# Routing from the raw residual: norm weights moved into the router's, the root into the selection, GpSimd multiplies x by the gain

## The chip, the cores and the metric

The kernel runs on one core of a Trainium2 chip. The metric is the device time in microseconds of one execution, as the median of several runs; lower is better. PE is TensorE (PEld its weight loads), DVE is VectorE, ACT is ScalarE, POOL is GpSimd, SP is SyncE, which issues most DMAs.

## The reference

Two layers on x (256 tokens x 1024, fp32). Layer 0: pooling mixer and dense SwiGLU. Layer 1: forgetting attention and a mixture of 8 experts, top 2. Each sub-layer has a norm before and one after.

```python
def rms_norm(x, g):
    return x * lax.rsqrt(jnp.mean(x * x, axis=-1, keepdims=True) + RMS_EPS) * g

def moe_swiglu(h, w_router, w_gate, w_up, w_down):
    logits = (h @ w_router).astype(jnp.float32)
    top_val, top_idx = lax.top_k(logits, 2)
    top_w = jax.nn.softmax(top_val, axis=-1)
    gates = jnp.sum(jax.nn.one_hot(top_idx, 8) * top_w[..., None], axis=-2)
    for e in range(8):                      # F_EXP = 3584
        out = out + gates[..., e:e + 1] * swiglu(h, w_gate[e], w_up[e], w_down[e])

# layer 1
x = x + rms_norm(forgetting_attention(rms_norm(x, g[1, 0]), ...), g[1, 1])
x = x + rms_norm(moe_swiglu(rms_norm(x, g[1, 2]), ...), g[1, 3])
```

## The kernel before

Tokens are two blocks (`tb`) of 128, one token a partition. Every engine runs its own program, written out by hand; engines wait for each other on counting semaphores. Weights come in units of 1 MB (128 x 2048 fp32) through a ring: 10 slots up to the experts, 14 with them. SP issues a unit's load when the unit that was in its slot has been used (`unit_used`, `b_used`). Products of most stages are made of three fp32r products: ACT copies a unit to its high part (`hi`, L620), DVE subtracts it from the unit for its low part (`lo`, L931), and PE multiplies high by high, high by low and low by high (`three`, L1413 to L1415). Activations are split likewise.

The experts are taken in four pairs. In a pair, expert A has up to 128 gathered tokens and works with the three products; expert B has up to 64 and works in plain fp32 (L1786, L1799) on unsplit units. A run over an expert is 42 units. SP's first 14 expert units are loaded ahead of the stage below (the last two when x is complete, `x_done` 6).

The stage that the change touches lies between attention and the first expert:

- `out_part` (PE) makes the attention's output in four PSUM banks, two halves of 512 columns for each block. `post_squares(5, tb)` (ACT) squares and sums them, `scale_bank` (DVE) multiplies by the gain, `root` (DVE, a chain of small linked instructions) makes the reciprocal root of the mean square, `add_normed` adds to x (`x_done`).
- `squares(6, tb)`, `root(6, tb)` and `norm_x(6, tb)` make the normed and weighted input `xn`; PE transposes it (`input_transposed(3, tb)`, L1435), ACT and DVE make `h_hi` and `h_lo`. DVE does block 0's `root(6, 0)` and `norm_x(6, 0)` ahead of block 1's post norm.
- The router: 24 products with `wr2` (weights split in high and low) as the stationary side and both blocks' tokens as the moving one give transposed logits, which DVE copies (L1238) and PE transposes back (L1721). DVE takes the top two, makes 0/1 matrices `m12` and `mboth`; PE counts ranks by products with constant matrices (L1727 to L1731); DVE writes `sel`, a 0/1 matrix of tokens by places (L1267), and PE gathers the first expert's tokens with it (`gather`, L1739), `xn` being the stationary side.
- ACT and DVE split the gathered tokens (`he_hi` L827, `he_lo` L1274). DVE then makes the table that orders the experts (`key` to `rtab_i`, L1280 to L1291), and GpSimd the places of all tokens and, once in each half of a pair, the next selection (`select`). GpSimd also loads the gains and clears `y`.
- `keep_warm(n)` (L1420) issues n products of 128 x 128 that nobody reads; the counts are in `WARM`.

Of the kernel before, what the change touches and what calls it, by code (L numbers as in the profile page):

```python
# [24 lines left out]
E = 8  # L25
# [25 lines left out]
SELECT_STEPS = 10  # L51
# [15 lines left out]
WARM = (16, 6, 10, 8, 28, 8, 8, 8)  # L67


def select(eng, ops, chain, before, gpos, gpos_next, step, gate, sel, sel2, gsel, iota, ready,  # L70
           ready_count, done, ALU):
# [15 lines left out]
    ops.tensor_tensor(sel[:, :, :], sel[:, :, :], sel2[:, :, :], ALU.add).then_inc(ready, 1)  # L87
    eng.wait_ge(ready, ready_count)
# [26 lines left out]
def trunk(nc, x_d, norm_g, pool_w, pool_scale, w_in, b_f, w_out, ffn_gate, ffn_up, ffn_down,  # L115
# [9 lines left out]
    with ExitStack() as ctx:  # L125
# [13 lines left out]
        xn = sb("xn", [P, TB, D])  # L139
        h_hi = sb("h_hi", [P, KB, T], f32r)  # L140
        h_lo = sb("h_lo", [P, KB, T], f32r)
# [26 lines left out]
        wr2 = sb("wr2", [P, KB, 2 * E], f32r)  # L168
# [72 lines left out]
        lgT = act[0:E, 0:T]  # L241
# [67 lines left out]
        lgT_psum = sem("lgT_psum")  # L309
        lgT_done = sem("lgT_done")  # L310
# [6 lines left out]
        pairs_done = sem("pairs_done")  # L317
        rank_copied = sem("rank_copied")
# [131 lines left out]
        def sq_at(n, tb):  # L450

            if n == 0:
                return tb + 1
            if n == 7:
                return 20 + 2 * tb + 2
            before, pre = 2 + 6 * ((n - 1) // 2), n % 2 == 0
            if n < 3:
                return before + (4 + tb + 1 if pre else 2 * tb + 2)
            return before + 3 * tb + (3 if pre else 2)
# [36 lines left out]
        def _(sp):  # L496
# [10 lines left out]
            for i, row in enumerate((norm_g[0, 0:1, :], pool_scale, norm_g[0, 1:2, :])):  # L507
# [11 lines left out]
                         w_router[0].rearrange("(k p) n -> p k n", p=P)).then_inc(small_in, 16)  # L519
            sp.dma_start(bf[:, :], b_f.rearrange("o h -> h o")).then_inc(small_in, 16)  # L520
# [94 lines left out]
        def _(sc):  # L615
# [9 lines left out]
            def squares(n, tb):  # L625

                if n:
                    sc.wait_ge(x_done, n - 2 + tb + 1)
                nc.scalar.activation(xn[:, tb, :], x[:, tb, :], ACT.Square,
                                     accum_out=sums[:, n, tb, 0:1]).then_inc(sq_done, 1)  # L630
# [67 lines left out]
            sc.wait_ge(small_in, 48)  # L698
            nc.scalar.activation(wf2[:, :, 0:H], small_w[:, :, 0:H], ACT.Copy).then_inc(small_hi, 1)
            nc.scalar.activation(wr2[:, :, 0:E], small_w[:, :, H:H + E], ACT.Copy).then_inc(small_hi, 1)  # L700
# [118 lines left out]
            sc.wait_ge(gap_done, 1)  # L819
            nc.scalar.activation(gtmp[:, :, 1:2], gtmp[:, :, 0:1], ACT.Exp).then_inc(gexp_done, 1)  # L820
            nc.scalar.activation(silu[:, 0:1], consts[:, C_ONES:C_ONES + 1], ACT.Silu)
# [8 lines left out]
            he_hi(0)  # L830
            hi(MOE_U0 + 3)
# [88 lines left out]
        def _(ve):  # L920
# [13 lines left out]
            def lo(u):  # L934
                split_lo(hi_slot(u), slot_of(u), u + 1 - WHOLE_UNITS)

# [138 lines left out]
            for i, (wide, at, n) in enumerate(((wf2, 0, H), (wr2, H, E))):  # L1075
                ve.wait_ge(small_hi, i + 1)
                nc.vector.tensor_tensor(wide[:, :, n:2 * n], small_w[:, :, at:at + n], wide[:, :, 0:n].bitcast(f32),
                                        ALU.subtract).then_inc(small_lo, 1)
# [72 lines left out]
            ve.wait_ge(small_in, 48)  # L1151
# [86 lines left out]
            nc.vector.tensor_copy(lgT, bank[4][0:E, 0:T]).then_inc(lgT_done, 1)  # L1238
            ve.wait_ge(lg_psum, 1)
            link(nc.vector.tensor_copy(lg[:, :, :], bank[5][:, 0:TB * E].rearrange("p (b e) -> p b e", e=E)))  # L1240
            for tb in range(TB):
                step = nc.vector.max(top[:, tb, :], lg[:, tb, :])
            link(step)
            for tb in range(TB):
                step = nc.vector.max_index(topi[:, tb, :], top[:, tb, :], lg[:, tb, :])
            link(step)
            link(nc.vector.tensor_copy(topf[:, :, :], topi[:, :, 0:2]))
            nc.vector.tensor_tensor(gtmp[:, :, 0:1], top[:, :, 1:2], top[:, :, 0:1], ALU.subtract).then_inc(gap_done, 1)
            for tb in range(TB):
                for i in range(2):  # L1250
                    step = nc.vector.tensor_scalar(m12[:, tb, i, :], iota8, topf[:, tb, i:i + 1], None, ALU.is_equal)
            link(step)
            nc.vector.tensor_tensor(mboth[:, :, :], m12[:, :, 0, :], m12[:, :, 1, :], ALU.add).then_inc(m_done, 1)
            ve.wait_ge(m_done, 1)
            link(nc.vector.tensor_scalar(away[:, :, :], mboth[:, :, 0:1], float(-2 * T), float(2 * T),
                                         ALU.mult, ALU.add))
            ve.wait_ge(gexp_done, 1)
            link(nc.vector.tensor_scalar(gtmp[:, :, 2:3], gtmp[:, :, 1:2], 1.0, None, ALU.add))
            link(nc.vector.reciprocal(gate[:, :, 0:1], gtmp[:, :, 2:3]))
            link(nc.vector.tensor_tensor(gate[:, :, 1:2], gate[:, :, 0:1], gtmp[:, :, 1:2], ALU.mult))  # L1260
# [3 lines left out]
            count = bank[5][:, TB * E:(TB + 1) * E]  # L1264
# [143 lines left out]
        def _(pe):  # L1408
# [276 lines left out]
            def out_part(w, tb):  # L1685
                hi, lo = weights(OUT_U0 + w, D)
                tok = slice(tb * P, (tb + 1) * P)
                for half in range(2):
                    cols = slice(half * HALF, (half + 1) * HALF)
                    for i in range(2):  # L1690
                        k = 2 * w + i
                        step = three(bank[(3, 7, 1, 2)[2 * tb + half]][:, :], o_hi[:, k, tok], o_lo[:, k, tok],
                                     hi[:, i, cols], lo[:, i, cols], k == 0, k == KB - 1)
                if w == 3 and tb == 0:
# [18 lines left out]
            keep_warm(WARM[2])  # L1713
            input_transposed(3, 0)
            keep_warm(WARM[4], to=bank[5])
            input_transposed(3, 1)
            pe.wait_ge(h_lo_done, h_at(3, 3))
            three_t(bank[4][0:E, 0:T], wr2, E).then_inc(lgT_psum, 1)
            pe.wait_ge(lgT_done, 1)
            for tb in range(TB):  # L1720
                step = nc.tensor.transpose(bank[5][:, tb * E:(tb + 1) * E], lgT[:, tb * P:(tb + 1) * P], ident[0:E, 0:E])  # L1721
            step.then_inc(lg_psum, 1)
            keep_warm(WARM[5])

            pe.wait_ge(m_done, 1)
# [3 lines left out]
            mm(bank[5][:, E:2 * E], before, mboth[:, 1, :], start=False, stop=True)  # L1729
            mm(bank[5][:, 2 * E:3 * E], ones, mboth[:, 0, :], start=True, stop=False)  # L1730
            mm(bank[5][:, 2 * E:3 * E], ones, mboth[:, 1, :], start=False, stop=True).then_inc(rank_psum, 1)  # L1731
# [315 lines left out]
```

## Time and profile before

| | |
|---|---|
| median of 3 runs | 1256.77 us (1255.49 to 1258.2) |
| profiled execution, its own time | 1253.61 us |
| its span, first to last instruction | 1251.8 us |
| mean granted TensorE clock | 0.991 |
| busy: PE, DVE, ACT, POOL | 1214.1, 689.2, 539.2, 119.9 us |
| DMA | 412.49 MB, 330 GB/s over the span |

The span lies within the execution's own time; the 1.8 us between them are outside the first and the last instruction. A busy engine is one with an instruction in work; matmuls overlap, so a full PE is not PE at its peak. The granted clock is the share of full speed that TensorE was given.

### The profile page before, as it was taken

How to read it: one execution, taken by the hardware profiler on the slowest of the kernel's cores; microseconds unless marked ns; L12 is line 12 of the kernel's file. 1: busy time of each engine (PE TensorE's matmuls, PEld its weight loads, DVE VectorE, ACT ScalarE, POOL GpSimd, SP SyncE). 2: the span in 40 equal slices, each digit the busy share in tenths (PEclk: the TensorE clock that was granted, in tenths of full speed). 3: DMA queues.
4: the chain of work that ended last, by engine and by line, in shares of the span. 5: the costliest groups of instructions: out<-in, count | busy, mean ns of one | idle time of the engine just before them, and what ended most of it. 6: DMA issues, size and time to landing. Idle time of an engine off the chain costs nothing.

```text
span 1251.8 us, 15496 instructions
## 1 busy us (share of the span) xinstructions
PE 1214.1 (97%) x6044; PEld 849.2 (68%) x6044; DVE 689.2 (55%) x770; ACT 539.2 (43%) x522; POOL 119.9 (10%) x131
## 2 busy tenths in 40 slices
PE   9999999989999999999899999999999989999996
PEld 7888887778877888534688843478883347887332
DVE  2854454656657989200788910188871028886102
ACT  2634344445535777100677600167750026775001
POOL 0000000000004350010005010000501000050100
PEclk8999999999999999999999999999999999999999
DMA  9755554573365999899999999999999999999995
GB/s 302 265 183 190 179 190 147 148 223 121 102 247 193 368 365 368 333 416 406 414 414 406 415 409 413 410 414 414 406 413 415 409 413 415 415 406 408 410 407 211
DMA packets 141292, 412.49 MB, mean 330 GB/s; under 512 B 9683, under 2 KB 29139, under 8 KB 141142
## 3 DMA queue, kind: packets, MB, share of 16 engines
q1 hardware_dynamic: 140406, 408.23, 85.6%
q0 software_dynamic: 816, 3.28, 0.8%
q8 instruction: 50, 0.82, 0.3%
q14 instruction: 20, 0.16, 0.0%
HBM read 410.44 MB, written 1.05 MB: 329 GB/s over the span
## 4 chain that ended last, share of the span: by engine, by line
PE 86%; DMA 5%; DVE 4%; SPq 2%; ACT 1%; issue 1%; DVEq 0%; ACTq 0%
PE bank L1413 19%; PE bank L1415 19%; PE bank L1414 19%; PE bank L1786 14%; DMA raw<-in_moe_w_gate 4%; PE bank L1799 4%; SPq L561 2%; PE bank L1739 1%; PE bank L1420 1%; DVE raw_lo L931 1%; PE bank L1862 1%; PE bank L1509 1%; PE bank L1816 1%; PE bank L1675 1%; DMA head_row<-in_heads 1%
## 5 line engine op out<-in xcount | busy, mean ns | idle before, releaser
L931 DVE TENSOR_TENSOR raw_lo<-raw,w_hi 128x2048 fp32r<-128x2048 f32 x149 | 340.4, 2301 | 81.1 <-ACT w_hi L620 80.7
L620 ACT ACTIVATE w_hi<-raw 128x2048 fp32r<-128x2048 f32 x149 | 284.4, 1916 | 125.7 <-PE bank L1415 73.7
L1413 PE MATMUL bank<-w_hi,h_hi 128*128 128x512 f32 x568 | 226.5, 399 | 13.4 <-DVE h_lo L1274 9.3
L1414 PE MATMUL bank<-raw_lo,h_hi 128*128 128x512 f32 x576 | 225.6, 392 | 0.0
L1415 PE MATMUL bank<-w_hi,h_lo 128*128 128x512 f32 x568 | 222.5, 392 | 0.0
L1786 PE MATMUL bank<-raw,h_b 128*64 128x512 f32 (+1 forms) x768 | 143.1, 523 | 0.0
L1413 PEld LDWEIGHTS bank<-w_hi,h_hi 128*128 128x128 f32 x568 | 106.9, 188 | 44.7 <-issue 15.5
L1414 PEld LDWEIGHTS bank<-raw_lo,h_hi 128*128 128x128 f32 x576 | 108.7, 189 | 21.8
L1415 PEld LDWEIGHTS bank<-w_hi,h_lo 128*128 128x128 f32 x568 | 107.1, 188 | 23.2
L931 DVE TENSOR_TENSOR raw_extra_lo<-raw_extra,w_hi 128x2048 fp32r<-128x2048 f32 x48 | 112.4, 2363 | 14.2 <-ACT w_hi L620 14.0
L1786 PEld LDWEIGHTS bank<-raw,h_b 128*64 128x64 f32 x768 | 53.6, 137 | 82.6 <-issue 74.6
L620 ACT ACTIVATE w_hi<-raw_extra 128x2048 fp32r<-128x2048 f32 x48 | 92.1, 1918 | 19.3 <-PE bank L1415 19.3
L887 ACT ACTIVATE silu<-bank 128x512 f32<-128x512 f32 (+1 forms) x16 | 8.7, 544 | 208.5 <-PE bank L1786 208.5
L1413 PE MATMUL bank<-w_hi,aT_hi 128*128 128x512 f32 x232 | 93.2, 402 | 0.0
L1415 PE MATMUL bank<-w_hi,aT_lo 128*128 128x512 f32 x232 | 91.6, 395 | 0.0
L1369 DVE COPY aT_b<-bank 128x512 f32<-128x512 f32 (+1 forms) x16 | 10.0, 625 | 141.3 <-PE bank L1870 141.3
L1799 PE MATMUL bank<-raw,aT_b 128*64 128x512 f32 x320 | 71.0, 593 | 0.5 <-DMA raw<-in_moe_w_down 0.5
L75 POOL TENSOR_TENSOR gpos_next<-gpos,slots_step 128x4 f32<-128x4 f32 x8 | 4.5, 568 | 670.6 <-PE bank L1809 670.6
L1365 DVE TENSOR_TENSOR act<-silu,bank 128x512 f32<-128x512 f32 (+1 forms) x16 | 9.9, 621 | 89.0 <-PE bank L1786 89.0
L1786 PE MATMUL bank<-raw_extra,h_b 128*64 128x512 f32 x256 | 57.4, 595 | 0.0
L1414 PE MATMUL bank<-raw_lo,aT_hi 128*128 128x512 f32 x144 | 57.0, 395 | 0.0
L1799 PEld LDWEIGHTS bank<-raw,aT_b 128*64 128x64 f32 x320 | 22.9, 137 | 45.0 <-issue 43.2
(315 smaller groups left out, 1617.6 us busy)
## 6 DMA issues: line engine op xcount, KB each, us to landing
raw<-in_moe_w_gate SPq DMA_DIRECT2D x96, 1024.0 KB, 16.0
raw<-in_moe_w_up SPq DMA_DIRECT2D x80, 1024.0 KB, 15.3
raw<-in_moe_w_down SPq DMA_DIRECT2D x64, 1024.0 KB, 14.2
raw_extra<-in_moe_w_down SPq DMA_DIRECT2D x48, 1024.0 KB, 16.1
raw_extra<-in_moe_w_up SPq DMA_DIRECT2D x32, 1024.0 KB, 13.1
raw_extra<-in_moe_w_gate SPq DMA_DIRECT2D x16, 1024.0 KB, 13.2
raw<-in_ffn_w_gate SPq DMA_DIRECT2D x11, 1024.0 KB, 5.2
raw<-in_ffn_w_up SPq DMA_DIRECT2D x11, 1024.0 KB, 5.2
```

Of the source, the lines that this page charges most:

```text
L561: sp.dma_start(blocks_of(raw_slot(s), n), src).then_inc(raw_in[s], 16)
L620: nc.scalar.activation(to, raw_slot(source), ACT.Copy).then_inc(hi_ready, 1)
L931: nc.vector.tensor_tensor(lo_slot(source), raw_slot(source), high.bitcast(f32), ALU.subtract).then_inc(lo_ready, 1)
L1413: mm(out, a_hi, b_hi, start=first, stop=False)
L1414: mm(out, a_hi, b_lo, start=False, stop=False)
L1415: return mm(out, a_lo, b_hi, start=False, stop=last)
L1420: mm(to[:, 0:P], source, source, start=True, stop=True)
L1509: step = mm(to[:, tb * FG:(tb + 1) * FG], h_whole[:, k, tok], weights_u[:, k, :], start=(k == 0), stop=(k == KB - 1))
L1675: mm(logits(i, b), qk[h0:h0 + HD, b * P:(b + 1) * P], qk[h0:h0 + HD, T:T + (b + 1) * P], start=True, stop=False)
L1739: step = mm(bank[6 + k * slots // HALF][:, at:at + slots], xn[:, tb, k * P:(k + 1) * P], sel[:, tb, 0:slots], start=(tb == 0), stop=(tb == 1))
L1786: step = mm(to[t * CAP_B:(t + 1) * CAP_B, 0:n], h_b[:, k, :], w[:, i, t * n:(t + 1) * n], start=(k == 0), stop=(k == KB - 1))
L1799: step = mm(bank[4][t * CAP_B:(t + 1) * CAP_B, :], aT_bs[s % 2][:, m * P + g * CAP_B:m * P + (g + 1) * CAP_B], w[:, i, t * HALF:(t + 1) * ...
```

## The change

- **Norm weights in the router's.** A new load brings the gain `norm_g[1, 2]` as a column for each block of 128 rows (`gain_t6`); DVE multiplies the router weights by it (`wr_g`), in place of splitting them into `wr2`.
- **Raw residual, by token.** PE transposes x itself, in quarters, as soon as each is there (`residual_transposed`); ACT copies them to `x_t`. The router is 8 fp32 products for each block with `x_t` as the stationary side, so that logits come out by token (`router`). DVE takes the top two for each block by itself (`top_two`). The reciprocal root is the same factor on all logits of a token and leaves their order; it enters the gap of the two logits and the selection matrices instead (`rstd` as second factor in `sel`, `factor` in `select`).
- **Post norm of the last block by halves.** For block 1, DVE scales, adds and signals the two halves of 512 columns one by one (`scaled_half`, `added_half`, semaphore `x_front`), ahead of anything of the next norm; `root(6)` is made once for both blocks, behind the top two.
- **GpSimd weighs x.** `xn` is now x times the gain, made by GpSimd, one instruction of 128 x 1024 for each block; `gather` waits for it.
- **Order.** ACT's `hi(MOE_U0)` comes first; `he_hi(0)` comes ahead of the exp. DVE splits unit `MOE_U0` by halves, and does units 1 and 2 ahead of the table, unit 3 behind it, the gate weights behind that. The count for the table comes in a bank of its own, with a signal of its own. `x_t` and `x_sq` lie in the memory of `h_hi` and `h_lo`.
- **Warming products.** 10 and 28 around the transposes go, 8 behind the router become 4.

```diff
-SELECT_STEPS = 10
+SELECT_STEPS = 11
-WARM = (16, 6, 10, 8, 28, 8, 8, 8)
+WARM = (16, 6, 0, 8, 0, 4, 8, 8)
...
 (select)
-    ops.tensor_tensor(sel[:, :, :], sel[:, :, :], sel2[:, :, :], ALU.add).then_inc(ready, 1)
-    eng.wait_ge(ready, ready_count)
+    ops.tensor_tensor(sel[:, :, :], sel[:, :, :], sel2[:, :, :], ALU.add).then_inc(chain, 1)
+    n += 1
+    eng.wait_ge(chain, before + n)
+    ops.tensor_tensor(sel[:, :, :], sel[:, :, :], factor, ALU.mult).then_inc(ready, 1)
...
 (SP)
+            sp.dma_start(gain_t6[:, :], norm_g[1, 2, :].rearrange("(k p) -> p k", p=P),
+                         allow_slow_non_contiguous=True).then_inc(small_in, 16)
             sp.dma_start(bf[:, :], b_f.rearrange("o h -> h o")).then_inc(small_in, 16)
...
 (ACT)
+            hi(MOE_U0)
             post_squares(5, 0, attn_out, (y0_psum, 3), in_xn, after=7)
-            squares(6, 0)
-            post_squares(5, 1, attn_out, (unit_used, MOE_U0), in_xn, after=9)
-
-            input_hi(3, [0])
-            squares(6, 1)
-            hi(MOE_U0)
-            input_hi(3, [1])
+            for half in range(2):
+                sc.wait_ge(*((out_half, 1), (unit_used, MOE_U0))[half])
+                nc.scalar.activation(in_xn(1, half), attn_out(1, half), ACT.Square,
+                                     accum_out=sums[:, 5, 1, half:half + 1]).then_inc(sq_done, 1)
+            def residual_copied(tb):
+                for b in (2 * tb, 2 * tb + 1):
+                    sc.wait_ge(tr_done, 4 * 3 + b + 1)
+                    nc.scalar.activation(input_part(x_t, 3, b), bank_blocks(3, b), ACT.Copy).then_inc(x_t_done, 1)
+            for tb in range(TB):
+                residual_copied(tb)
+                squares(6, tb)
             for j in range(1, 3):
                 hi(MOE_U0 + j)
...
 (DVE)
+            nc.vector.tensor_tensor(wr_g[:, :, :], small_w[:, :, H:H + E],
+                                    gain_t6[:, :, None].to_broadcast([P, KB, E]), ALU.mult).then_inc(small_lo, 1)
...
             add_normed(5, 0, v)
-            root(6, 0)
-            norm_x(6, 0)
-            scale_bank(5, 1, v, attn_out, (unit_used, MOE_U0), True)
+            scaled_half(0)
             root(5, 1)
-            scaled_ready()
-            add_normed(5, 1, v)
-            input_lo(3, [0])
-            root(6, 1)
-            norm_x(6, 1)
-            input_lo(3, [1])
-            lo(MOE_U0)
-            ve.wait_ge(lgT_psum, 1)
-            nc.vector.tensor_copy(lgT, bank[4][0:E, 0:T]).then_inc(lgT_done, 1)
...
+            added_half(0)
+            scaled_half(1)
+            added_half(1)
+            def top_two(tb):
+                ve.wait_ge(lg_psum, tb + 1)
+                link(nc.vector.tensor_copy(lg[:, tb, :], bank[4 + tb][:, 0:E]))
+                link(nc.vector.max(top[:, tb, :], lg[:, tb, :]))
+                link(nc.vector.max_index(topi[:, tb, :], top[:, tb, :], lg[:, tb, :]))
...
+            top_two(0)
+            lo_half(MOE_U0, 0)
+            top_two(1)
+            root(6, 0, TB)
...
-                nc.vector.tensor_scalar(sel[:, tb, :], iota, pos0[:, tb, :], None,
-                                        ALU.is_equal).then_inc(sel_ready, 1)
-            lo(MOE_U0 + 1)
+                nc.vector.tensor_scalar(sel[:, tb, :], iota, pos0[:, tb, :], rstd[:, 6, tb:tb + 1],
+                                        ALU.is_equal, ALU.mult).then_inc(sel_ready, 1)
+            lo_half(MOE_U0, 1)
...
             he_lo(0, halves=[0])
+            lo(MOE_U0 + 1)
+            he_lo(0, halves=[1])
+            lo(MOE_U0 + 2)
+            ve.wait_ge(rank_psum, 2)
...
-            he_lo(0, halves=[1])
+            lo(MOE_U0 + 3)
             nc.vector.tensor_copy(rank[:, :, :], rank_ps).then_inc(rank_copied, 1)
-            lo(MOE_U0 + 2)
-            lo(MOE_U0 + 3)
...
 (PE)
-            keep_warm(WARM[2])
-            input_transposed(3, 0)
-            keep_warm(WARM[4], to=bank[5])
-            input_transposed(3, 1)
-            pe.wait_ge(h_lo_done, h_at(3, 3))
-            three_t(bank[4][0:E, 0:T], wr2, E).then_inc(lgT_psum, 1)
-            pe.wait_ge(lgT_done, 1)
+            def residual_transposed(tb):
+                for i in range(2):
+                    pe.wait_ge(*((x_done, 5), (x_done, 5), (x_front, 1), (x_done, 6))[2 * tb + i])
+                    for k in range(4):
+                        c = (4 * i + k) * P
+                        step = nc.tensor.transpose(bank[input_bank(3, 2 * tb + i)][:, k * P:(k + 1) * P],
+                                                   x[:, tb, c:c + P], ident)
+                    step.then_inc(tr_done, 1)
+            def router(tb):
+                for k in range(KB):
+                    if k % 4 == 0:
+                        pe.wait_ge(x_t_done, 2 * tb + k // 4 + 1)
+                    step = mm(bank[4 + tb][:, 0:E], x_t[:, k, tb * P:(tb + 1) * P], wr_g[:, k, :], start=(k == 0),
+                              stop=(k == KB - 1))
+                step.then_inc(lg_psum, 1)
             for tb in range(TB):
+                residual_transposed(tb)
+                router(tb)
             keep_warm(WARM[5])
...
             keep_warm(WARM[3])
+            pe.wait_ge(xn_done, 4)
             gather(2, CAP)
...
 (GpSimd)
+                if n == 6:
+                    po.wait_ge(gain_in[0], 32)
+                    for tb in range(TB):
+                        po.wait_ge(x_done, 5 + tb)
+                        if tb == 1:
+                            po.wait_ge(x_front, 1)
+                        nc.gpsimd.tensor_tensor(xn[:, tb, :], x[:, tb, :], gain[:, 0, :], ALU.mult).then_inc(xn_done, 1)
```

## Rows read from the trace of the kernel before

**Rows 1.** Windows: us; busy PE, PEld, DVE, ACT, POOL; PEclk, DMA share, GB/s.

```profile
362.00:378.00 16.00, 11.76 (x101) 10.94 (x100) 12.82 (x38) 8.63 (x14) 2.38 (x3) 1.00 1.01 393
380.00:392.00 12.00, 11.38 (x88) 10.58 (x87) 8.80 (x37) 2.89 (x5) 0.56 (x3) 1.00 0.00 0
396.00:503.00 107.00, 107.00 (x479) 87.14 (x478) 95.47 (x60) 78.88 (x52) 37.64 (x28) 1.00 1.00 369
513.00:594.00 81.00, 81.00 (x416) 31.87 (x418) 8.42 (x13) 3.16 (x6) 5.67 (x12) 1.00 1.02 404
```

**Rows 2.** Chain that ended last: start, us, what.

```profile
360.26 1.29 DVE x L979
...
365.69 0.69 DVE v L994
...
366.40 0.70 ACT xn L639 x2
...
369.03 1.28 DVE x L979
...
373.25 1.29 DVE xn L974
...
377.26 0.28 PE bank L1413
...
384.34 1.89 PE bank L1420 x16
386.23 3.57 PE bank L1739 x32
389.80 0.30 PE bank L1413
```

**Rows 3.** Timeline of PE: start, us, what, idle before.

```profile
361.94 0.40 PE L1415 MATMUL bank<-w_hi,o_lo 128*128 128x512 f32 x1
...
374.59 1.09 PE L1435 MATMUL bank<-consts,xn 128*128 128x128 f32 x8 [1.42 <-DVE xn L974]
...
383.31 0.37 PE L1728 MATMUL bank<-mboth,consts 128*128 128x8 f32 x2
```

**Rows 4.** Timeline of ACT, 362 to 368 us.

```profile
362.63 0.58 ACT L639 ACTIVATE xn<-bank 128x512 f32<-128x512 f32 x1
...
366.99 1.07 ACT L655 ACTIVATE h_hi<-bank 128x512 fp32r<-128x512 f32 x2
```

**Rows 5.** Timeline of DVE, 381 to 394 us.

```profile
381.00 0.17 DVE L1240 COPY lg<-bank 128x16 f32<-128x16 f32 x1 [0.38 <-PE bank L1721]
...
382.83 0.17 DVE L1253 TENSOR_TENSOR mboth<-m 128x16 f32<-128x16 f32 x1
...
384.64 0.48 DVE L1267 TENSOR_SCALAR sel<-consts,pos 128x128 f32<-128x128 f32 x2
...
391.84 2.29 DVE L931 TENSOR_TENSOR raw_lo<-raw,w_hi 128x2048 fp32r<-128x2048 f32 x1
```

**Rows 6.** Timeline of POOL, 414 to 415 us.

```profile
414.26 0.40 POOL L1986 TENSOR_TENSOR sel<-sel,gate 128x128 f32<-128x128 f32 x1
414.74 0.74 POOL L1989 TENSOR_TENSOR gsel<-gsel,sel 128x256 f32<-128x256 f32 x1
```

**Rows 7.** Timeline of DVE, 414 to 418 us.

```profile
414.20 0.67 DVE L1340 TENSOR_TENSOR h_b<-aT_b,bank 128x512 f32<-128x512 f32 x1
414.80 2.83 DVE L931 TENSOR_TENSOR raw_extra_lo<-raw_extra,w_hi 128x2048 fp32r<-128x2048 f32 x1
```

**Rows 8.** Timelines of SP's queue and of ACT, start of the kernel.

```profile
4.73 0.67 SPq L512 DMA_DIRECT2D gain_t<-in_norm_g  x1
...
41.93 1.92 ACT L620 ACTIVATE w_hi<-raw 128x2048 fp32r<-128x2048 f32 x1
```

**Rows 9.** PE's granted clock (PEclk) in a stretch, columns of Rows 1.

```profile
12.00:14.00 2.00, 2.00 (x3) 0.66 (x2) 1.72 (x4) 0.78 (x2) 0.00 (x0) 0.50 1.13 285
```

**Rows 10.** Timeline of PE, 15 to 19 us.

```profile
15.00 3.78 PE L1420 MATMUL bank<-silu 128*128 128x128 f32 x16
```

More of the change, by code:

```diff
@@ L66, with select @@
 WARM_START = 14
-WARM = (16, 6, 10, 8, 28, 8, 8, 8)
-def select(eng, ops, chain, before, gpos, gpos_next, step, gate, sel, sel2, gsel, iota, ready,
-           ready_count, done, ALU):
+WARM = (16, 6, 0, 8, 0, 4, 8, 8)
+def select(eng, ops, chain, before, gpos, gpos_next, step, gate, factor, sel, sel2, gsel, iota, ready, done, ALU):
     ops.tensor_tensor(gpos_next[:, :, :], gpos[:, :, :], step, ALU.subtract).then_inc(chain, 1)
@@ L139, in trunk @@
         xn = sb("xn", [P, TB, D])
+        with nc.sbuf_tensor("x_t", [P, KB, T], f32) as x_t:
+            pass
         h_hi = sb("h_hi", [P, KB, T], f32r)
+        with nc.sbuf_tensor("x_sq", [P, TB, D], f32) as x_sq:
+            pass
         h_lo = sb("h_lo", [P, KB, T], f32r)
@@ L628, in squares @@
                     sc.wait_ge(x_done, n - 2 + tb + 1)
-                nc.scalar.activation(xn[:, tb, :], x[:, tb, :], ACT.Square,
+                if n == 6 and tb == 1:
+                    sc.wait_ge(x_front, 1)
+                nc.scalar.activation((x_sq if n == 6 else xn)[:, tb, :], x[:, tb, :], ACT.Square,
                                      accum_out=sums[:, n, tb, 0:1]).then_inc(sq_done, 1)
@@ L830, in _ @@
             he_hi(0)
+            sc.wait_ge(gap_done, 1)
+            nc.scalar.activation(gtmp[:, :, 1:2], gtmp[:, :, 0:1], ACT.Exp).then_inc(gexp_done, 1)
+            nc.scalar.activation(silu[:, 0:1], consts[:, C_ONES:C_ONES + 1], ACT.Silu)
             hi(MOE_U0 + 3)
@@ L935, in lo, with lo_half @@
                 split_lo(hi_slot(u), slot_of(u), u + 1 - WHOLE_UNITS)
+            def lo_half(u, half):
+                cols = slice(half * (UNIT // 2), (half + 1) * (UNIT // 2))
+                ve.wait_ge(hi_ready, u + 1 - WHOLE_UNITS)
+                step = nc.vector.tensor_tensor(lo_slot(slot_of(u))[:, cols], raw_slot(slot_of(u))[:, cols],
+                                               hi_slot(u)[:, cols].bitcast(f32), ALU.subtract)
+                if half == 1:
+                    step.then_inc(lo_ready, 1)
             def root(n, first, blocks=1):
@@ L1240, in _ @@
[L1240 to L1248, printed above, removed]
@@ L1249, in _, with scaled_half, added_half @@
-            for tb in range(TB):
+            def scaled_half(half):
+                cols = slice(half * HALF, (half + 1) * HALF)
+                ve.wait_ge(sq_done, sq_at(5, 1) - 1 + half)
+                nc.vector.tensor_tensor(v[:, 1, cols], attn_out(1, half), gain[:, 1, cols],
+                                        ALU.mult).then_inc(yg_done, 1)
+                yg[0] += 1
+            def added_half(half):
+                cols = slice(half * HALF, (half + 1) * HALF)
+                scaled_ready()
+                nc.vector.scalar_tensor_tensor(x[:, 1, cols], v[:, 1, cols], rstd[:, 5, 1:2], x[:, 1, cols], ALU.mult,
+                                               ALU.add).then_inc((x_front, x_done)[half], 1)
@@ L1250, in _ @@
                 for i in range(2):
                     step = nc.vector.tensor_scalar(m12[:, tb, i, :], iota8, topf[:, tb, i:i + 1], None, ALU.is_equal)
-            link(step)
-            nc.vector.tensor_tensor(mboth[:, :, :], m12[:, :, 0, :], m12[:, :, 1, :], ALU.add).then_inc(m_done, 1)
-            ve.wait_ge(m_done, 1)
+                link(step)
+                nc.vector.tensor_tensor(mboth[:, tb, :], m12[:, tb, 0, :], m12[:, tb, 1, :],
+                                        ALU.add).then_inc(m_done, 1)
@@ L1255, in _ @@
+            top_two(0)
+            lo_half(MOE_U0, 0)
+            top_two(1)
+            root(6, 0, TB)
+            ve.wait_ge(m_done, 2)
             link(nc.vector.tensor_scalar(away[:, :, :], mboth[:, :, 0:1], float(-2 * T), float(2 * T),
                                          ALU.mult, ALU.add))
-            ve.wait_ge(gexp_done, 1)
-            link(nc.vector.tensor_scalar(gtmp[:, :, 2:3], gtmp[:, :, 1:2], 1.0, None, ALU.add))
-            link(nc.vector.reciprocal(gate[:, :, 0:1], gtmp[:, :, 2:3]))
@@ L1292, in _ @@
                                     ALU.add).then_inc(pairs_done, 1)
-            he_lo(0, halves=[1])
+            lo(MOE_U0 + 3)
             nc.vector.tensor_copy(rank[:, :, :], rank_ps).then_inc(rank_copied, 1)
-            lo(MOE_U0 + 2)
-            lo(MOE_U0 + 3)
+            ve.wait_ge(gexp_done, 1)
+            link(nc.vector.tensor_scalar(gtmp[:, :, 2:3], gtmp[:, :, 1:2], 1.0, None, ALU.add))
+            link(nc.vector.reciprocal(gate[:, :, 0:1], gtmp[:, :, 2:3]))
+            nc.vector.tensor_tensor(gate[:, :, 1:2], gate[:, :, 0:1], gtmp[:, :, 1:2], ALU.mult).then_inc(gates_done, 1)
             def order_table():
@@ L1693, in out_part @@
                                      hi[:, i, cols], lo[:, i, cols], k == 0, k == KB - 1)
+                    if w == 3 and tb == 1 and half == 0:
+                        step.then_inc(out_half, 1)
                 if w == 3 and tb == 0:
```

54 lines of the change are left out of this document (27 added, 27 removed).

## The prediction

> **What bounds the kernel now.** I read the page first: PE is busy for 97% of the span, so the share of busy time settles nothing, and neither does DMA, whose slices are full as well. The windows by stage [rows 1] part the kernel. The last routing stretch (362 to 378 us) has DMA full at 393 GB/s while it fills the ring of 14 units; from 380 to 392 us DMA stands still, because all 14 slots are full and no expert unit has been used. In the first run over an expert of 128 tokens (396 to 503 us) DMA moves 369 GB/s, below the 404 of the stretch after it: it waits for slots that PE frees. So the end of the kernel hangs on the moment at which PE starts the first expert. Everything behind it shifts with it, as long as the ring is full by then: the 12 us without a byte say that up to 12 us can be taken from the stage before DMA takes over as the limit. A start earlier by so many us is worth the same at the end.
>
> What sets that start is in the chain in order of time [rows 2]. The residual of block 0 is ready at 361.55 (360.26 + 1.29), but block 1's at 370.31 only, since DVE does block 0's second root and norm first and takes up block 1 at 365.69, though PE's last product ended at 362.34 [rows 3]. Then come block 1's root and norm (to 374.54), transposes, high and low halves, 24 router products from 377.26, logits back through a transpose, selection, ranks, 8 warming products (384.34 to 386.23), of which the last 1.1 us are waited for though the selection is there at 385.12 (384.64 + 0.48 [rows 5]), the gather at 386.23, and the first expert product at 389.80.
>
> **The new path, step by step, first as if nothing interfered.**
> 1. Block 1's first half is out of PE six products, about 1.4 us, before 362.34. Its square is done before 362. The second half's square takes 0.70 [rows 2] behind 362.34: 363.1. ACT's split of the first expert unit (1.92 [rows 8]) moves ahead of block 0's squares, into ACT's wait for PE; if it came late it would cost what is over, at most 1.9.
> 2. The root takes 1.93 (366.40 + 0.70 to 369.03): 365.0. Adding half a block, estimated at 0.75 (the whole takes 1.29): first half at 365.8. Scaling the second half 0.7, adding 0.75: residual ready at 367.2 instead of 370.31.
> 3. Four transposes take 0.45 to 0.6 (eight take 1.09 [rows 3]), a copy 0.6 [rows 4]: 368.5. A small fp32 product comes every 0.22 us [rows 3]; eight for block 1 end at 369.6. Block 0's transposes, copies and products lie before 366. This replaces norm, high and low halves, 24 products, the copy of the transposed logits and its two transposes.
> 4. The old selection of both blocks took 2.0 (381.00 to 383.00 [rows 5]); by block I put 1.5. Block 0: 367.2 to 368.8; half of unit 0's split, 1.15 (half of 2.29 [rows 5]); block 1: to 371.5.
> 5. PE: ranks 5 x 0.22 plus its tail, 372.8; eight warming products 1.89 [rows 2], 374.7. DVE: root over both blocks, two steps more and one less than 1.93, so 2.1; two small steps 0.4; selection matrices 0.48: 374.45. The gather starts at 374.7: 11.5 us earlier.
>
> **GpSimd weighs x.** 128 elements take it 0.40, 256 take 0.74 [rows 6], which gives 2.7 for 1024 (estimate). The first weighing runs from 361.65 to 364.4, the second from x's completion; neither makes the gather wait, since even behind 368.6 it ends at 371.4. Its price is on DVE. A subtraction of two SBUF tensors on DVE took 2.83 instead of 2.29 where it met GpSimd's 256-element add; a DVE product that reads PSUM met a GpSimd product and took its usual 0.67 [rows 6, 7]. The root's first step is an addition of two SBUF values and is due at 363.1: held until 364.4, it moves all behind it by 1.3 us, the residual to 368.5. The second weighing (368.6 to 371.3) then meets the small steps of block 0's selection, the last of which adds two SBUF tensors. Held until 371.3, then 0.2, half the split (372.7), block 1 (374.2), ranks and warming 3.2: gather at 377.4. The lower bound of this cost is nothing, the upper 2.7; I take 2.7, because the nearest rows show the delay to be nearly the whole overlap. That leaves 8.8.
>
> The Trainium skill (GPSIMD Engine Reference, Key points) says that GpSimd shares its SBUF interfaces with VectorE and contends with instructions that read two SBUF inputs; it speaks against this change, and the two rows agree with it. The same reference (side-by-side cycle accounting) has 4.5 us for 2048 elements of a two-input operation; by it one weighing would take 2.25, and the sum would come out about 1 us earlier.
>
> **Given back at the start of the expert.** DVE keeps less lead now: counted from the gather's start, token halves (2.6 until the first is copied, 0.67), unit 1 (2.2), second token half (0.67), unit 2 (2.2), the table of experts (ten small steps, 1.9), unit 3 (2.2): 12.4. PE wants unit 3 at 3.57 [rows 2] + 3 x 2.7 = 11.6 (a unit is 12 products at 107.00/479 = 0.223 [rows 1]). The stall is 0.8, and 0.2 for unit 4, behind which the gate weights stand: 1.0. Bounds: 0 if the table is quicker, 2 if GpSimd's table steps also hold DVE. DVE catches up by 0.5 per unit after that (2.2 against 2.7), and PE's lost time is not made up, as PE is the limit there.
>
> **What costs nothing.** The router weight product in place of a subtraction, one ACT copy less, and one more load of 4 KB on SP's queue: its twin took 0.67 to issue [rows 8]. It is queued ahead of the forget bias and the second and later weight units; ACT takes the first of these at 41.93 and waits for no DMA there. Without that cover it costs 0.7. The last gain's load, GpSimd's clearing of y and the table work queue behind the weighing; the first is wanted at the kernel's end, the others only in the second quarter of the first expert. The added multiply in each selection (0.74 [rows 6], eight times) lies well ahead of its gather, on an engine that waits for PE at either end; its cover gone, it would cost 0.7 a time. ACT's exp comes behind the token halves; its next split waits for PE anyway.
>
> **Sum.** 11.5 - 2.7 - 1.0 = 7.8 earlier. The profiled execution took 1253.6 us, so 1245.8 for it; the median shown is 1256.8, from which I take the same 7.8: 1249.0.
>
> **Rivals.**
> - *Interference is small.* GpSimd's weighing leaves DVE's small steps alone. Then 11.5 - 1.0 = 10.5: 1246.3. For it: no row shows a step of one or two elements being held. Against it: the whole subtraction was held. Chance 0.15.
> - *TensorE's clock falls in the stage.* The 10 and 28 warming products around the transposes are gone; between 363.4 and the next transposes (365.8 to 367.1) PE has only products of 8 columns. Over 12 to 14 us it stood at 0.50, the 1.2 GHz level, after a run of products of one row [rows 9]; in the whole of the old stage it was at 1.00, the 2.4 GHz level [rows 1]. At the lower level 16 records take 3.78 [rows 10] against 1.89 [rows 2]. Ranks + 1.1, warming + 1.9, other + 0.5: 3.5 given back, so 1252.5; with the whole gather slow another 3.6, so 1256.1, no change. Chance 0.27, of which 0.07 for the second.
> - *Slower: the lower level lasts into the first expert.* Then every unit costs 2.7 more. Behind 3.5 + 3.6 there is 0.7 of gain left; from 1.2 units on it is slower by over 0.2%. Three units give 1256.1 + 8.1 = 1264. Against it: the warming products and the gather keep PE full for more than 5 us before. Chance 0.06.
> - *The start isn't what counts.* If DMA were the limit already in the first expert (its busy share is 1.00 there [rows 1]), the earlier start would be lost: 1256.8. Against it: its rate is 369 against 404, and DMA's own restart moves with PE's first used unit. Chance 0.06.
>
> **How the numbers follow.** The forecast has 0.46. The range goes from 1245 (no interference and no stall, 1245.3) to 1255 (clock down for part of the gather, 1.5 for the spread of runs); it leaves out most of the last three tails. The likeliest case alone is 1247.5 to 1250.5. Faster by over 0.2%, about what a measurement of this kernel can tell from none (2.5 us): 0.46 + 0.15 + 0.20 and half of what is between, 0.83. Within: 0.10. Slower: 0.07.
>
> **What would show it.** In the changed trace: residual of block 1 ready at about 368.5; GpSimd's two products about 2.7 us each, and a root whose first step starts when the first of them ends; logits of block 1 before 371.5; gather at about 377.4, first expert product near 381; two short waits of PE for DVE's low halves at units 3 and 4; DMA's pause between the filled ring and the first used unit short of 12 us by what was gained; the rounds behind it as long as before. The forecast is wrong if PE's granted clock is below 1.00 in that stage, if DVE rather than PE sets the gather's start by much, or if the first round is longer than before.

## The result and the profile after

The changed kernel took 1261.82 us (median of 20 runs, 1255.63 to 1263.78), the kernel before, run beside it, 1255.42 (median of 20, 1247.79 to 1258.79). The ratio is 1.005, 95% interval 1.0036 to 1.0064: slower by half a per cent, where 1249.0 and faster was forecast. The profiled span is 1257.1 us.

The windows of the changed kernel, columns as in [rows 1]; the stage now lies some 3 us earlier in this execution, because attention ended at 359.7 instead of 362.3:

```profile
360.00:376.00 16.00, 12.96 (x68) 11.93 (x67) 14.41 (x46) 8.28 (x12) 6.16 (x5) 0.59 1.00 396
...
389.00:496.00 107.00, 106.48 (x476) 86.41 (x475) 97.23 (x66) 78.52 (x52) 48.52 (x36) 1.00 1.00 367
506.00:587.00 81.00, 79.99 (x405) 30.71 (x404) 8.43 (x13) 3.16 (x6) 6.25 (x13) 1.00 1.02 397
```

Two things differ from [rows 1]. TensorE's granted clock is 0.59 on average from 360 to 376 us, where it was 1.00. And in the stretch of expert B DMA moves 397 GB/s where it moved 404, with the same busy share of 1.02: the transfers are slower, not fewer.

The chain of the changed kernel through the stage (start, us, what):

```profile
359.76 0.70 ACT xn L823 x2
360.48 0.97 DVE sums L971
...
363.18 0.75 DVE x L1263
...
364.57 0.75 DVE x L1263
...
365.91 1.89 DVE topf L1277
367.82 2.38 DVE m L1279 x2
...
375.24 3.61 PE bank L1459 x16
378.85 2.38 PE bank L1790 x16
...
389.44 2.21 DVE raw_lo L948
391.69 0.50 PE bank L1452
```

The new path is there as drawn up, with three small VectorE steps that take 1 to 2.4 us instead of 0.16 to 0.37: `sums`, `topf` and the pair that makes `m`. GpSimd's timeline has what ran beside them:

```profile
359.05 2.37 POOL L1994 TENSOR_TENSOR xn<-x,gain 128x1024 f32<-128x1024 f32 x1 [105.66 <-DVE x L1004]
365.40 2.36 POOL L1994 TENSOR_TENSOR xn<-x,gain 128x1024 f32<-128x1024 f32 x1 [3.99 <-DVE x L1263]
...
368.29 1.86 POOL L2002 MEMSET y<- 128x1024 f32 x2
```

Each held step ends within 0.05 us of one of these: the addition of `sums` at 361.43 with the first weighing (361.42), the cast of `topf` at 367.79 with the second (367.76), the two compares that make `m12` (`m` in the views) at 370.18 with the clearing of `y` (370.15).

Now the same stages in all profiled executions, worked out from the timelines. "Stage" runs from the last attention product to the first product of the first expert; a round is from the first product of a pair to that of the next; the ratio is to the kernel before as it was measured beside each.

| kernel | last attention product to gather | stage | rounds 1, 2, 3 | rest | span | ratio, 95% interval |
|---|---|---|---|---|---|---|
| before | 23.7 | 27.3 | 209.7, 214.9, 214.9 | 222.7 | 1251.8 | |
| changed | 18.9 | 23.1 | 212.2, 217.6, 217.6 | 227.0 | 1257.1 | 1.005, 1.0036 to 1.0064 |
| e1_same_places | 19.0 | 22.9 | 210.4, 214.9, 214.9 | 225.3 | 1250.9 | 0.9988, 0.9969 to 1.0008 |
| e2_pad32 | 19.0 | 23.0 | 211.7, 217.6, 217.6 | 226.8 | 1257.8 | 1.0046, 1.0028 to 1.0065 |
| e3_before_pad32 | 23.7 | 27.3 | 212.1, 217.4, 217.6 | 225.6 | 1259.4 | 1.0072, 1.0048 to 1.0096 |
| e4_places_warm | 16.3 | 20.0 | 211.2, 214.9, 214.8 | 223.6 | 1241.3 | 0.9954, 0.9936 to 0.9973 |
| e5_before_256 | 23.8 | 27.3 | 208.4, 212.7, 213.4 | 223.5 | 1247.1 | 0.9984, 0.9963 to 1.0004 |
| e6_before_pad128 | 25.2 | 28.8 | 210.4, 217.5, 217.6 | 225.3 | 1263.6 | 1.0077, 1.0054 to 1.01 |
| e7_after_256 | 16.3 | 20.0 | 209.3, 211.5, 212.0 | 221.9 | 1237.6 | 0.9911, 0.9885 to 0.9937 |
| e8_clear_early | 14.4 | 18.0 | 209.1, 214.0, 212.9 | 223.6 | 1234.6 | 0.9898, 0.9877 to 0.992 |
| e9_weigh_dve | 14.1 | 17.7 | 209.4, 212.0, 211.4 | 222.0 | 1235.9 | 0.9896, 0.987 to 0.9921 |

So the change shortened its stage by 4.2 us and lengthened what lies behind it: 2.5 and twice 2.7 us in the rounds and 4.3 in the rest, 12.2 in all, in code that it hardly touched. That is 8.0 us longer from the last attention product on; the spans differ by 5.3 because attention ended 2.6 us earlier in the profiled execution of the changed kernel (over all profiled executions it ended between 356.8 and 364.0), and the medians differ by 6.4. The windows from 1060 to 1140 us, in the middle of the last run over an expert of 128 tokens, first of the kernel before, then of the changed one:

```profile
1060.00:1140.00 80.00, 80.00 (x362) 65.25 (x361) 70.49 (x39) 59.37 (x40) 16.60 (x12) 1.00 1.03 411
```

```profile
1060.00:1140.00 80.00, 80.00 (x362) 65.37 (x361) 70.81 (x39) 59.11 (x41) 19.12 (x13) 1.00 1.03 406
```

PE is full in both and does the same number of products, so nothing is lost here at once. It is lost at the end of the round, where PE has caught up with DMA. Windows at the end of the third round, first before, then changed, and under each the transfer that stands there in the chain of work that ended last:

```profile
1000.00:1030.00 30.00, 25.74 (x162) 12.99 (x159) 5.48 (x7) 6.27 (x7) 0.00 (x0) 1.00 1.03 412
...
1006.73 17.37 DMA raw<-in_moe_w_gate
```

```profile
1000.00:1030.00 30.00, 24.71 (x158) 12.06 (x154) 4.42 (x6) 5.21 (x6) 0.00 (x0) 1.00 1.03 406
...
1007.16 18.00 DMA raw<-in_moe_w_gate
```

PE is idle for 4.3 of the 30 us before and for 5.3 after, and the chain that ended last runs through a transfer in both. A round moves 84 units of 1 MB, 88.1 million bytes: over 214.9 us that is 410 GB/s, over 217.6 it is 405. The rounds go by DMA's rate, and went by it before the change.

The rest, behind the third round, has a second part. In the changed kernel the last expert's last product ends 2.1 us later, counted from the start of that round, and the remaining 2.2 us lie behind it. There PE waits for 3.44 us ahead of its last eight products, first of the kernel before, then of the changed one:

```profile
1240.21 1.99 PE L1925 MATMUL bank<-ye,gselT 64*128 64x512 f32 x8 [1.30 <-ACT ye L899]
```

```profile
1245.52 2.43 PE L1977 MATMUL bank<-ye,gselT 64*128 64x512 f32 x8 [3.44 <-issue]
```

"issue" says that the profile shows nothing that PE waited for. Of the kernels below, e1 has such a wait too (3.18 us), and so has e3 (2.15), which is the kernel before with 32 unused bytes; e4, with the changed kernel's instructions there, has 0.72. So the change alone doesn't make it, and what does is open.

Why is the rate lower? What the change does to memory suggested it. `wr2` (512 bytes of a partition) is replaced by `wr_g` (256) and `gain_t6` (32), so every tile allocated behind it lies 224 bytes lower. Among them are the four ring slots of `raw_extra`, which move from byte 196352, 256 x 767, to 196128, 32 above a multiple of 256. The other ten slots, `raw`, lie in front of it and stay at 16512, 128 above a multiple. Slots are 8192 bytes apart, so all slots of a group lie alike. The time between the landings of one unit and the next, by slot (medians over 600 to 1200 us, from the trace's DMA events; the boundary between the two groups blurs by one slot):

| kernel | `raw` starts at (over a multiple of 256) | us per unit | `raw_extra` starts at (over) | us per unit | GB/s, 1060 to 1140 us |
|---|---|---|---|---|---|
| before, e1, e4 | 16512 (128) | 2.55 to 2.57 | 196352 (0) | 2.43 to 2.49 | 411 |
| changed | 16512 (128) | 2.56 | 196128 (32) | 2.56 | 406 |
| e2 | 16512 (128) | 2.56 | 196160 (64) | 2.56 | 406 |
| e3 | 16512 (128) | 2.56 | 196384 (32) | 2.56 | 406 |
| e6 | 16512 (128) | 2.56 | 196480 (128) | 2.56 | 406 |
| e5, e7 | 16640 (0) | 2.48 to 2.52 | 196352 (0) | 2.48 to 2.52 | 418 |

The unused bytes of the experiments below move every tile behind them, not `raw_extra` alone. That it is `raw_extra` rests on this table: only the units of slots that moved changed their time.

### The profile page after: what moved, and what is told of

Read it like the earlier page. It is cut to its first block, busy times and chain, and to the rows that moved or that the text cites. A ratio compares the mean times of both kernels' runs of the same rounds, so it can differ in the third digit from the quotient of the medians.

```text
span 1257.1 us, 15344 instructions
## 1 busy us (share of the span) xinstructions
PE 1212.5 (96%) x5966; PEld 846.6 (67%) x5966; DVE 689.1 (55%) x762; ACT 539.0 (43%) x521; POOL 141.1 (11%) x141
## 3 DMA queue, kind: packets, MB, share of 16 engines
HBM read 410.44 MB, written 1.05 MB: 327 GB/s over the span
## 4 chain that ended last, share of the span: by engine, by line
PE 85%; DMA 6%; DVE 4%; SPq 2%; ACT 1%; issue 1%; DVEq 0%; ACTq 0%
PE bank L1452 19%; PE bank L1454 19%; PE bank L1453 19%; PE bank L1838 13%; DMA raw<-in_moe_w_gate 4%; PE bank L1851 4%; SPq L570 2%; DVE raw_lo L948 2%; DMA raw_extra<-in_moe_w_down 1%; PE bank L1459 1%; PE bank L1790 1%; PE bank L1914 1%; PE bank L1548 1%; PE bank L1868 1%; PE bank L1714 1%
## 5 line engine op out<-in xcount | busy, mean ns | idle before, releaser
L1452 PE MATMUL bank<-w_hi,h_hi 128*128 128x512 f32 x568 | 227.2, 400 | 14.4 <-DVE h_lo L1307 9.9
L948 DVE TENSOR_TENSOR raw_extra_lo<-raw_extra,w_hi 128x2048 fp32r<-128x2048 f32 x48 | 113.1, 2377 | 14.2 <-ACT w_hi L629 14.0
## 6 DMA issues: line engine op xcount, KB each, us to landing
raw<-in_moe_w_down SPq DMA_DIRECT2D x64, 1024.0 KB, 14.2
```

Of the source, the lines that this page charges most:

```text
L948: nc.vector.tensor_tensor(lo_slot(source), raw_slot(source), high.bitcast(f32), ALU.subtract).then_inc(lo_ready, 1)
L1452: mm(out, a_hi, b_hi, start=first, stop=False)
```

## The experiments

**e1_same_places**: the changed kernel with 224 unused bytes, so that all later tiles lie where they lay before.

```diff
         gain_t6 = sb("gain_t6", [P, KB])
+        pad = sb("pad", [P, 56])
```

> The changed kernel with an unused tile of 224 bytes behind gain_t6, so that every later tile lies where it lay in the kernel before (raw_extra at 196352 bytes of a partition instead of 196128). Theory P (the places of the tiles set DMA's rate in the expert rounds): its packets of 4096 bytes in the rounds go back from 164 ns to a mix of 159 and 164, a round from 217.6 to 214.9 us, and the time to about 1252, 3 below the kernel before, because the first expert starts some 4 us earlier in its stage and loses 1. Theory R (the routing itself costs, by GpSimd's longer selections or the stalls of the first expert): nothing changes against the changed kernel, 1261.8.

Measured: 1252.84 us, 9.0 less than the changed kernel; rounds 2 and 3 of 214.9 as before, in a kernel whose instructions are those of the changed one. All that these two had lost comes back with 224 bytes of nothing; round 1 stays 0.7 longer than before and the rest 2.6, with PE's wait of 3.18 us at the end in it. The stage stays at 22.9, 4.4 shorter than before, but the time can't be told from the kernel before: 2.3 us less by medians, with an interval from 3.9 faster to 1.0 slower.

**e2_pad32**: the same with 32 bytes in place of 224 (`[P, 8]`), which puts `raw_extra` on a multiple of 64.

> The changed kernel with an unused tile of 32 bytes behind gain_t6: raw_extra at 196160, a multiple of 64 again, but not the place that it had before. Theory P in the form of alignment to 64 bytes: as the kernel with the old places, about 1252, packets partly at 159 ns. Theory P in the form of a certain address, or theory R: 1261.8, all packets at 164 ns.

Measured: 1260.09, rounds 2 and 3 of 217.6. A multiple of 64 does nothing; this form of the theory falls.

**e3_before_pad32**: the kernel before, with 32 unused bytes.

```diff
         wr2 = sb("wr2", [P, KB, 2 * E], f32r)
+        pad = sb("pad", [P, 8])
```

> The kernel before with an unused tile of 32 bytes behind wr2: raw_extra at 196384, 32 bytes off a multiple of 64, and the routing untouched. Theory P (alignment): slower by about 10 us, 1265, all packets of the rounds at 164 ns, a round 217.6. Theory R: no change, 1255.4.

Measured: 1262.22, slower by 0.7%, from 32 bytes that nobody reads. Its window from 1060 to 1140 us:

```profile
1060.00:1140.00 80.00, 80.00 (x362) 65.31 (x361) 71.00 (x39) 58.68 (x40) 16.59 (x12) 1.00 1.03 406
```

**e4_places_warm**: e1 with TensorE kept at work in the stage, to part the clock's share from the rest.

```diff
-WARM = (16, 6, 0, 8, 0, 4, 8, 8)
+WARM = (16, 6, 0, 8, 0, 18, 8, 8)
 (residual_transposed)
                 for i in range(2):
+                    if tb == 1 and i == 1:
+                        keep_warm(3)
 (router)
+                    if tb == 0 and k < KB - 1:
+                        keep_warm(1)
                 step.then_inc(lg_psum, 1)
+                if tb == 0:
+                    keep_warm(4)
```

> The changed kernel with the old places and warming products put back where PE waits in the routing stage: one behind each of block 0's first seven router products, 4 behind them, 3 between block 1's two quarters, 18 instead of 4 behind the router. If the clock's fall to the 1.2 GHz level at about 363 us is what held the stage up, the granted clock stays at 1.00, ranks, warming products and gather take 6.8 instead of 9.9 us, and the kernel is 3 us faster than the same without them. If DVE's steps set the stage's length, at most 0.5.

Measured: 1248.87, ratio 0.9954; stage 20.0, 2.9 shorter than e1's. The granted clock (the third number from the end), first of the changed kernel from 362 to 378 us, then of e4 over its whole stage:

```profile
362.00:364.00 2.00, 0.95 (x10) 0.86 (x9) 1.79 (x8) 0.46 (x2) 0.00 (x0) 0.72 1.00 403
364.00:378.00 14.00, 12.40 (x55) 11.71 (x56) 12.42 (x37) 5.83 (x6) 4.75 (x4) 0.50 0.85 340
```

```profile
357.00:377.00 20.00, 19.52 (x170) 19.05 (x169) 16.82 (x50) 9.00 (x13) 6.33 (x5) 1.00 0.79 320
```

At 0.50, the 1.2 GHz level, the 16 records of `keep_warm` ahead of the gather took 3.61 us and the router's eight products 3.42; at the upper level the latter had taken 1.95 for block 0. In the changed kernel the clock fell at 362.9, as block 0's products of 8 columns ended and a wait of 1.05 us for x began; in e1, with the same instructions, it fell at 368.5, 6.0 us behind attention instead of 3.2. All three holds are in e4 as they were; two of them:

```profile
363.07 1.87 DVE L1278 CAST topf<-topi 128x2 f32<-128x2 uint32 x1
364.98 2.38 DVE L1280 TENSOR_SCALAR m<-consts,topf 128x8 f32<-128x8 f32 x2
```

**e5_before_256**: the kernel before with `sums` (128 bytes) allocated ahead of `raw` instead of behind it, so that all 14 slots start at multiples of 256. The tiles between the two places move by 128 bytes with it.

> The kernel before, with its tile sums (128 bytes) allocated ahead of raw instead of behind: raw moves from 16512 to 16640 bytes, a multiple of 256; raw_extra stays at 196352, which is one already. Theory M (DMA writes faster into slots that start at a multiple of 256): in the traces so far a unit lands every 2.44 to 2.49 us in raw_extra's slots where it lies at 196352, and every 2.56 in all others; the ten raw slots come to about 2.45 too, a round from 214.9 to 208 us, the time to about 1235. Theory H (high addresses, or something else of raw_extra): no change, 1255.

Measured: 1251.12 against 1254.32, and this window:

```profile
1060.00:1140.00 80.00, 80.00 (x360) 65.08 (x359) 70.99 (x39) 58.88 (x40) 16.59 (x12) 1.00 1.03 418
```

The forecast of about 1235 is missed, and the time by itself shows no gain (ratio 0.9984, interval 0.9963 to 1.0004). The rate shows one, of the wrong size: the ten slots of `raw` went from 2.56 to 2.49 us per unit, not to the 2.45 that `raw_extra` had alone, and `raw_extra` itself now takes 2.49.

**e6_before_pad128**: the kernel before with 128 unused bytes behind `wr2`; `raw_extra` at a multiple of 128.

> The kernel before with an unused tile of 128 bytes behind wr2: raw_extra at 196480, a multiple of 128 but not of 256. Theory M with 256: as with 32 bytes, about 1262, a unit every 2.56 us in all slots. If 128 is enough for raw_extra: 1255, with 2.44 to 2.49 us there.

Measured: 1263.38, rounds of 217.5, 406 GB/s. 128 bytes are no better than 32 or 64. Its stage is longer by 1.5; in this execution the clock was down for 3.4 us from 378.8 on.

**e7_after_256**: e4 with `sums` ahead of `raw`.

> The changed kernel with the old places, the warming products put back, and sums ahead of raw, so that raw and raw_extra both start at multiples of 256. Theory M: the gains add up, 1248.9 less 20, 1229. Otherwise 1249. If PE becomes the bound in the later rounds, the gain on this kernel is smaller than on the kernel before.

Measured: 1241.07, ratio 0.9911, where 1229 was forecast. The same stage as e4, rounds shorter by 1.9, 3.4 and 2.8 us. A unit takes 2.49 in all slots, as in e5, and not the 2.44 to 2.49 that the forecast had carried over from `raw_extra`.

**e8_clear_early**: e7 with GpSimd's clearing of `y` between the two weighings instead of behind them, and 10 warming products behind the router instead of 18.

```diff
 (GpSimd, from behind the loop over gains to here)
                     for tb in range(TB):
+                        if tb == 1:
+                            po.wait_ge(unit_used, MOE_U0)
+                            for b in range(TB):
+                                nc.gpsimd.memset(y[:, b, :], 0.0).then_inc(acc_done, 1)
                         po.wait_ge(x_done, 5 + tb)
```

> As the kernel before it in this list, with GpSimd's clearing of y between its two weighings instead of behind them, and 10 instead of 18 warming products behind the router. In the changed kernel's trace DVE's two comparisons for block 0 took 2.4 us instead of 0.4 while GpSimd cleared y. Theory C (clearing holds DVE's comparisons): they take 0.4, the gather and all behind it come 2.0 us earlier. Rival: the comparisons are held by the second weighing or something else, or the clearing now holds the root: no gain.

Measured: 1239.95. VectorE's timeline:

```profile
357.73 1.00 DVE L972 TENSOR_TENSOR sums<-sums 128x1 f32<-128x1 f32 x1 [0.67 <-ACT xn L824]
...
363.21 1.87 DVE L1278 CAST topf<-topi 128x2 f32<-128x2 uint32 x1
365.11 0.45 DVE L1280 TENSOR_SCALAR m<-consts,topf 128x8 f32<-128x8 f32 x2
```

The compares are free (0.45 instead of 2.38) and the stage is 2.0 shorter (1.9 to the gather). The 8 warming products fewer can't have done it alone: in e7 they ended at 376.08 and block 1's `mboth` was there at 376.12 only. The time is 1.1 below e7's, which the intervals don't part.

**e9_weigh_dve**: e8 with both weighings on VectorE.

```diff
 (GpSimd)
-                        nc.gpsimd.tensor_tensor(xn[:, tb, :], x[:, tb, :], gain[:, 0, :], ALU.mult).then_inc(xn_done, 1)
...
 (DVE)
             scaled_half(0)
+            weighed(0)
             root(5, 1)
...
             top_two(0)
-            lo_half(MOE_U0, 0)
+            weighed(1)
...
-            lo_half(MOE_U0, 1)
+            lo(MOE_U0)
```

> This is e8_clear_early with the two products x times gain made by VectorE instead of GpSimd: block 0's right behind the scaling of block 1's first half (where VectorE waited 0.67 us), block 1's in place of the first half of unit 0's split, whose two halves then come together behind the selection. GpSimd keeps only the clearing of y there. Theory (GpSimd's products hold VectorE's small steps for 0.85 and 1.7 us, so giving them to GpSimd gains next to nothing): the addition of sums and the cast of topf take 0.16 to 0.17 each again, the VectorE products 1.29 each, of which the first costs 0.6 and the second 0.1; from the last attention product to the first expert product 16.2 us instead of 18.0. VectorE's lead into the expert is 1.1 shorter, so the time falls by 0.7 to 1.8: about 1238.5 where e8 has 1240. Rival 1 (GpSimd's product is worth its price): the small steps are held by the clearing of y as well or the products cost their 1.29 in full, 18.5 us or more, and the time is that of e8 or above it by 1 us. Rival 2 (the shorter lead takes it all back): 16.2 us in the stage, but the first round is longer by 1.8 us and the time is that of e8.

Measured: 1241.1, ratio 0.9896, no different from e8. VectorE's timeline:

```profile
364.48 0.15 DVE L972 TENSOR_TENSOR sums<-sums 128x1 f32<-128x1 f32 x1
...
369.11 0.21 DVE L1286 CAST topf<-topi 128x2 f32<-128x2 uint32 x1
...
369.86 1.23 DVE L1272 TENSOR_TENSOR xn<-x,gain 128x1024 f32<-128x1024 f32 x1
372.47 0.17 DVE L1283 COPY lg<-bank 128x8 f32<-128x8 f32 x1 [1.38 <-PE bank L1778]
```

Both steps are quick again, so the weighings had held them. But the stage is 17.7 instead of the 16.2 expected: VectorE now waits 1.38 us for block 1's logits. With the holds gone PE is what is late, and by the warming products that e4 put in: the first half of block 1's x is there at 367.13, and PE takes it up at 368.98, behind them. With fewer warming products there the stage might have shrunk; that was not tried.

## Why the prediction was wrong

- **The step that failed** is "everything behind it shifts with it", with its check "the rounds behind it as long as before". The rounds grew by 2.5 to 2.7 us each. e1 and e3 show the cause from both sides: the places of tiles behind `wr2`, given back in the changed kernel and spoilt in the one before. By the profiles of the changed kernel and e1 it is 1.8 + 2.7 + 2.7 + 1.7 = 8.9 us; their medians differ by 9.0. The other 3.3 of the 12.2 us are in e1 too (0.7 in round 1, 2.6 in the rest) and don't come from the places. No rival named it. The prediction read the replacement of `wr2` for its instructions, not for its bytes.
- **"PE is the limit there"** failed with it. It came from the windows of a full PE in the middle of an expert. The end of a round shows the other side: PE idle for 4.3 of 30 us with a transfer in the chain, before the change already. The rival that the start isn't what counts was turned down on the first expert's 369 GB/s; by the end of the first round PE waits for DMA (3.1 us in the kernel before), and the two later rounds go by DMA. The start still counts, since DMA's restart moves with it: the queue of the weight units stood still for 14.2 us in the kernel before (the prediction's 12 lie within that), 10.5 in the changed one and 6.7 in e4.
- **The new path, 11.5 less 2.7 held.** The mechanism was right. From the last attention product to the first expert product 18.7 us were forecast (362.3 to 381), 20.0 came with the clock held up (e4), 23.1 as the change stood. The residual of block 1 was ready 5.6 us behind attention (forecast 6.2).
- **GpSimd's price** was mis-sized in its parts: a weighing takes 2.37, not 2.7 (its own two rows give 2.8), and the two hold 0.8 and 1.7 us, 2.5 for the 2.7 that were forecast. What was costed at nothing, the clearing of `y` behind the weighing, held 2.0 more; in e8, where it lies elsewhere, that is gone. The Trainium skill (GPSIMD Engine Reference, Key points) names, beside two SBUF inputs, a two-port mode of VectorE as contending; the cast and the compares have one input each and were held, which agrees if they ran in that mode, and no run shows the mode. Moving the weighings back to VectorE (e9) takes the holds of 0.8 and 1.7 us away and changes the time by nothing that can be measured; but PE was late there by its warming products, so e9 doesn't settle which engine is the better one.
- **The clock** was a rival with 0.27 and a price of 3.5. It fell, and costs 2.9 us of the stage (e1 to e4); it was up again at 380.0, before the first expert's first product at 382.8, so that the rival in which the lower level lasts into the expert did not come. The kernel is slower for a reason that no rival had.
- **The stall** of 1.0: PE stands still for 0.4 at unit 3 in the changed kernel. In e4, with neither the shift of tiles nor the fall of the clock, the stage is 7.3 shorter than before, round 1 is 1.5 and the rest 0.9 longer, which leaves 4.9; its ratio of 0.9954 is 5.8 us. What makes the remaining 1.1 of round 1 is open; the queue of the weight units stands still for 3.1 us at the change to expert B there, and for 2.2 in the kernel before. So the forecast gain of 7.8 would still have been off by 2 to 3. The clearing of `y` is 2.0, but that this nearly fills the gap is partly luck: without it the stage would have been 0.7 shorter than forecast (18.0 in e8 for 18.7), and round 1 was 0.5 longer than the stall allowed.

## What to carry to other kernels

When a change alters the size of any tile, list the byte offset of every tile behind it that DMA writes to, and judge the change with those offsets unchanged (an unused tile will do); here 32 bytes cost 0.7% (e3), and the whole redesign of a stage won 0.5% even with the places given back and the clock kept up (e4). Start the slots of a weight ring at multiples of 256 bytes: the rate rose from 411 to 418 GB/s with it, though e5's time alone doesn't show a gain. Read the end of a round as well as its middle before calling PE the limit. Before work is put on GpSimd "for free", list VectorE's small steps beside it, and count clearings too; and when warming products are taken out, keep enough of them that the next run of products doesn't start at the lower clock.

The best version here (e8: the change, tiles at multiples of 256, warming kept, clearing moved) takes 0.9898 of the kernel before, 0.9877 to 0.992; e9 is no different, and part of it, the multiples of 256, could be had without the change.

## What the runs showed of the hardware

- **Where a transfer lands sets its rate.** 1 MB units, 8192 bytes to a partition and moved mostly in packets of 4096, take 2.56 us each where the slots start 32, 64 or 128 bytes above a multiple of 256, and 2.49 where all start at one: 406 against 418 GB/s. The Trainium skill (DMA: Bandwidth & Descriptors, How a descriptor splits into AXI transactions) says of reads that every transaction of a descriptor must start at a multiple of 256 bytes, so that one that starts off such a multiple also fetches bytes that it does not use. An estimate from its count of beats makes 4096 bytes dearer by 1 in 128 at an offset of 32 and by 4 in 128 at 128. These runs show a price for the start of the written side, and it is about 2.8% at 32, 64 and 128 alike, which that count does not give.
- **Open:** with only `raw_extra` at such multiples its units took 2.43 to 2.49, with all slots there 2.48 to 2.52. All these starts are odd multiples of 256; larger powers of two were not tried. Why PE waits for up to 3.4 us before its last products in some profiles is open too.
- **Small VectorE steps can be held by GpSimd until its instruction ends.** Held: an addition of two values a partition beside the product (1.00 instead of 0.16), a cast (1.87 instead of 0.17), a compare of 8 columns beside the clearing (2.38 for two instead of 0.37). Not held beside the clearing: the same addition (0.15 in e9, with the clearing from 363.50 to 365.34), the product of 1024 (1.22) and the one-column steps of the root.
